# All 390 transposes on TensorE read and write through float32r views instead of float32

## The reference, cut to what matters

```python
def _conformer_layer(x, norm_g, w_in, dw_w, dw_b, ln_g, ln_b, w_out):
    h = _rms_norm(x, norm_g)
    a, b, z = jnp.split(h @ w_in, 3, axis=-1)
    y = _depthwise_causal_conv(a * jax.nn.sigmoid(b), dw_w, dw_b)
    y = jax.nn.silu(_layer_norm(y, ln_g, ln_b))
    return x + (y * jax.nn.silu(z)) @ w_out
...
def _diff_layer(x, k, v, ...):
    u = _rms_norm(x, norm_g) @ w_in
    q = _rms_norm(u[..., :DIFF_QK]...) ; z = u[..., DIFF_QK:]
    o = _rms_norm(_diff_attention(q, k, v, lam), subln_g) * (1.0 - lam_init)
    return x + (o * jax.nn.silu(z)) @ w_out
...
def hybrid_layer(x, cos, sin, ...):
    proj = rms_norm(x, pre_norm_w) @ w_in
    o_a = stick_breaking_attention(...) ; o_b = chunk_causal_softmax_attention(...)
    y = jnp.concatenate([o_a * silu(sb_gate), o_b * silu(mla_gate)], -1) @ w_out
    return x + rms_norm(y, post_norm_w)
```

## Time and profile before

| | |
|---|---|
| Time, median of 3 runs | 1269.71 us (1269.62 to 1270.36) |
| Span of the profiled execution | 1267.8 us |
| TensorE busy in it | 1259.6 us, 99% |
| Weight loads busy | 1052.1 us, 83% |
| VectorE, ScalarE, GpSimd busy | 791.8, 766.9, 204.6 us |
| Mean granted TensorE clock | 0.999 of full speed |

### The profile page before, as it was taken

The page is one execution under the profiler, slowest core; times in us unless marked ns, Lnnn a source line. Parts: engine busy times, 40 slices in busy tenths (PEclk is TensorE's granted clock), DMA queues, the critical chain, the costliest instruction groups (busy, mean ns, idle before and its releaser), DMA issues.

```text
span 1267.8 us, 16054 instructions
## 1 busy us (share of the span) xinstructions
PE 1259.6 (99%) x5936; PEld 1052.1 (83%) x5936; DVE 791.8 (62%) x1284; ACT 766.9 (60%) x1208; POOL 204.6 (16%) x148
## 2 busy tenths in 40 slices
PE   9999999999999999999999999999999999999998
PEld 8888888888888888888888888889988888888886
DVE  5498898476556665446677765555544445676545
ACT  5798798764557554445566674446644455666543
POOL 1499998900000000000000000000000000000000
PEclk9999999999999999999999999999999999999999
DMA  9898998944566666666555455567655556655563
GB/s 349 268 256 248 267 257 241 264 157 144 179 192 183 185 186 193 191 193 185 165 155 160 151 165 184 183 191 174 182 160 157 162 154 185 195 167 153 182 195 134
DMA packets 133564, 243.85 MB, mean 192 GB/s; under 512 B 12144, under 2 KB 22512, under 8 KB 133360
## 3 DMA queue, kind: packets, MB, share of 16 engines
q1 hardware_dynamic: 129600, 229.40, 58.2%
q0 software_dynamic: 3600, 13.11, 5.3%
q10 hardware_dynamic: 288, 0.32, 0.1%
HBM read 227.60 MB, written 2.10 MB: 181 GB/s over the span
## 4 chain that ended last, share of the span: by engine, by line
PE 97%; DVE 1%; ACT 1%; issue 0%; DVEq 0%; ACTq 0%
PE PS L1561 29%; PE PS L1563 29%; PE PS L1562 29%; PE PS L1494 3%; PE PS L1505 2%; PE PS L1690 1%; PE PS L1584 0%; PE PS L1586 0%; PE PS L1585 0%; PE PS L1623 0%; PE PS L1784 0%; PE PS L1754 0%; PE PS L1766 0%; PE PS L1643 0%; PE PS L1606 0%; PE PS L1612 0%
## 5 line engine op out<-in xcount | busy, mean ns | idle before, releaser
L1017 DVE TENSOR_TENSOR w_lo<-w_raw,w_hi 128x1024 fp32r<-128x1024 f32 (+1 forms) x339 | 411.1, 1214 | 354.0 <-ACT w_hi L549 353.1
L549 ACT ACTIVATE w_hi<-w_raw 128x1024 fp32r<-128x1024 f32 (+1 forms) x383 | 401.8, 1051 | 368.0 <-PE PS L1563 352.3
L1561 PE MATMUL PS<-w_hi,actB_hi 128*128 128x512 f32 (+1 forms) x752 | 298.8, 397 | 0.0
L1561 PE MATMUL PS<-w_hi,actA_hi 128*128 128x512 f32 x756 | 296.3, 392 | 0.0
L1563 PE MATMUL PS<-w_hi,actA_lo 128*128 128x512 f32 x756 | 294.6, 390 | 0.0
L1562 PE MATMUL PS<-w_lo,actA_hi 128*128 128x512 f32 x756 | 294.2, 389 | 0.0
L1563 PE MATMUL PS<-w_hi,actB_lo 128*128 128x512 f32 (+1 forms) x752 | 291.1, 387 | 0.0
L1562 PE MATMUL PS<-w_lo,actB_hi 128*128 128x512 f32 (+1 forms) x752 | 290.4, 386 | 0.0
L1563 PEld LDWEIGHTS PS<-w_hi,actA_lo 128*128 128x128 f32 x756 | 141.9, 188 | 30.1
L1561 PEld LDWEIGHTS PS<-w_hi,actA_hi 128*128 128x128 f32 x756 | 141.9, 188 | 29.3 <-DVE actA_lo L1032 0.3
L1562 PEld LDWEIGHTS PS<-w_lo,actA_hi 128*128 128x128 f32 x756 | 142.0, 188 | 29.1
(11 more groups left out here) (258 smaller groups left out, 1131.1 us busy)
## 6 DMA issues: line engine op xcount, KB each, us to landing
w_raw<-in_a_w_in SPq DMA_DIRECT2D x95, 512.0 KB, 5.7
w_raw<-in_w_in SPq DMA_DIRECT2D x88, 512.0 KB, 3.7
w_raw<-in_w_kv SPq DMA_DIRECT2D x64, 512.0 KB, 3.8
w_raw<-in_b_w_in SPq DMA_DIRECT2D x64, 512.0 KB, 3.7
w_raw<-in_a_w_out SPq DMA_DIRECT2D x32, 512.0 KB, 3.7
w_raw<-in_b_w_out SPq DMA_DIRECT2D x32, 512.0 KB, 3.7
w_raw<-in_w_out SPq DMA_DIRECT2D x32, 512.0 KB, 4.2
tap_products<-tap_products POOLq DMA_DIRECT2D x25, 512.0 KB, 8.3
```

The lines of the kernel that those rows point to most:

```text
L549: nc.scalar.activation(split_slot(u)[0], w_raw[:, RAW_SLOT[u], 0:2 * w], ACT.Copy)\
L1017: V.tensor_tensor(wl, w_raw[:, RAW_SLOT[u], 0:2 * w], wh.bitcast(F32), ALU.subtract)\
L1561: T.matmul(bank, ah, wh[:, kk, :], start=first and kk == 0, stop=False)
```

## The change

`ident_r`, a float32r copy of the identity, is made by GpSimd right behind the identity, and the wait ahead of unit 0 asks for it too. Each buffer that is turned gets a second name of type float32r at the same address (a tensor that is opened and closed right before the real one, or a slice of `aux_r`). All transposes go through `turn`, which reads the float32r names and writes PSUM through a float32r view. Number, shape, order and waits of TensorE's instructions are as before.

```diff
+        with nc.sbuf_tensor("x_res_r", [P, TT, D], F32R) as x_res_r:
+            pass
         x_res = sb("x_res", [P, TT, D])
...
         ident = sb("ident", [P, P])
+        ident_r = sb("ident_r", [P, P], F32R)
...
+            pool.wait_ge(S["ident_ready"], 1)
+            chain.tensor_copy(ident_r[:, :], ident[:, :]).then_inc(S["ident_ready"], 1)
             chain.memset(strict[:, :], 1.0)
...
+            def turn(out, src):
+
+                return T.transpose(out.bitcast(F32R), src, ident_r[:, :])
+
             def transpose_chunk(name, src, tiles=range(4)):
...
-                        ins = T.transpose(PS[:, 4 + i // 2, at:at + P], src(tok, i), ident[:, :])
+                        ins = turn(PS[:, 4 + i // 2, at:at + P], src(tok, i))
...
             def staged(buf):
-                return lambda tok, i: stage[:, buf, tok, i * P:(i + 1) * P]
+                return lambda tok, i: stage_r[:, buf, tok, i * P:(i + 1) * P]
...
-            pe.wait_ge(S["ident_ready"], 1)
+            pe.wait_ge(S["ident_ready"], 2)
...
-                            ins = T.transpose(PS[:, 6, i * P:(i + 1) * P], work[:, 0, i * P:(i + 1) * P],
-                                              ident[:, :])
+                            ins = turn(PS[:, 6, i * P:(i + 1) * P], work_r[:, 0, i * P:(i + 1) * P])
```

More of the change, by code:

```diff
@@ L263, in hybrid_program @@
         sb("w_raw_room", [P, RAW, 2 * NC])
+        with nc.sbuf_tensor("heads_out_r", [P, 4, TT, 2 * DH], F32R) as heads_out_r:
+            pass
         heads_out = sb("heads_out", [P, 4, TT, 2 * DH])
@@ L266, in hybrid_program @@
         w_lo = sb("w_lo", [P, PARTS, 2 * NC], F32R)
+        with nc.sbuf_tensor("stage_r", [P, 2, TT, NC], F32R) as stage_r:
+            pass
         stage = sb("stage", [P, 2, TT, NC])
+        with nc.sbuf_tensor("work_r", [P, 2, 384], F32R) as work_r:
+            pass
         work = sb("work", [P, 2, 384])
@@ L299, in hybrid_program @@
         conv = view(KT * (PAD + SEQ), KT, SEQ)
+        conv_r = aux_r[:, KT * (PAD + SEQ):KT * (PAD + 2 * SEQ)].rearrange("p (a b) -> p a b", a=KT)
         x_t = conv
         z_late = view(0, 2 * TT, NC)
+        z_late_r = aux_r[:, 0:2 * TT * NC].rearrange("p (a b) -> p a b", a=2 * TT)
         taps = view(KT * (PAD + 2 * SEQ), KT, TAPS)
@@ L317, in hybrid_program @@
         qu_stage = heads_out[:, 0:2, :, :].rearrange("p a b c -> p (a b c)").rearrange("p (t n) -> p t n", t=TT)
+        qu_stage_r = heads_out_r[:, 0:2, :, :].rearrange("p a b c -> p (a b c)").rearrange("p (t n) -> p t n", t=TT)
         qu_tmp = heads_out[:, 2:4, :, :].rearrange("p a b c -> p a (b c)")
@@ L1510, in staged @@
             def staged(buf):
-                return lambda tok, i: stage[:, buf, tok, i * P:(i + 1) * P]
+                return lambda tok, i: stage_r[:, buf, tok, i * P:(i + 1) * P]
             def rows(j):
-                return lambda tok, i: x_res[:, tok, j * NC + i * P:j * NC + (i + 1) * P]
+                return lambda tok, i: x_res_r[:, tok, j * NC + i * P:j * NC + (i + 1) * P]
             source = {}
@@ L1642, in _ @@
                             for i in range(4):
-                                ins = T.transpose(PS[:, 4 + tok, i * P:(i + 1) * P],
-                                                  conv[:, 4 * j + i, tok * P:(tok + 1) * P], ident[:, :])
+                                ins = turn(PS[:, 4 + tok, i * P:(i + 1) * P],
+                                           conv_r[:, 4 * j + i, tok * P:(tok + 1) * P])
                             ins.then_inc(S["stats_full"], 1)
@@ L1656, in _ @@
                     transpose_chunk(f"z{j}", staged(j) if j < 2 else
-                                    lambda tok, i: z_late[:, 2 * (j - 2) + tok, i * P:(i + 1) * P])
+                                    lambda tok, i: z_late_r[:, 2 * (j - 2) + tok, i * P:(i + 1) * P])
                 if C_OUT <= JUST_DONE.get(u - 2, 0) < C_K:
@@ L1694, in _ @@
                     pe.wait_ge(S["d_gated"], 2 * (j + 1))
-                    transpose_chunk(f"og{j}", lambda tok, i: heads_out[:, (2 * j + i // 2) % 4, tok,
-                                                                       (i % 2) * P:(i % 2 + 1) * P])
+                    transpose_chunk(f"og{j}", lambda tok, i: heads_out_r[:, (2 * j + i // 2) % 4, tok,
+                                                                         (i % 2) * P:(i % 2 + 1) * P])
                 if C_OUTB <= JUST_DONE.get(u - 2, 0) < C_CQ:
@@ L1708, in _ @@
                     for tok in range(TT):
-                        T.transpose(PS[0:ROT, 5, tok * P:(tok + 1) * P], stage[:, 1, tok, 256:320], ident[:, :])
+                        turn(PS[0:ROT, 5, tok * P:(tok + 1) * P], stage_r[:, 1, tok, 256:320])
                     for i in range(2):
@@ L1712, in _ @@
                             at = i * SEQ + tok * P
-                            ins = T.transpose(PS[:, 4, at:at + P], stage[:, 1, tok, i * P:(i + 1) * P],
-                                              ident[:, :])
+                            ins = turn(PS[:, 4, at:at + P], stage_r[:, 1, tok, i * P:(i + 1) * P])
                     ins.then_inc(S["t_full"], 1)
@@ L1722, in _ @@
                                 at, f = pair * SEQ + tok * P, (2 * j + pair) * P
-                                ins = T.transpose(PS[:, 4, at:at + P], qu_stage[:, tok, f:f + P], ident[:, :])
+                                ins = turn(PS[:, 4, at:at + P], qu_stage_r[:, tok, f:f + P])
                         ins.then_inc(S["t_full"], 1)
@@ L1748, in _ @@
                         for i in range(3):
-                            ins = T.transpose(PS[:, 7, i * P:(i + 1) * P], work[:, h % 2, i * P:(i + 1) * P],
-                                              ident[:, :])
+                            ins = turn(PS[:, 7, i * P:(i + 1) * P], work_r[:, h % 2, i * P:(i + 1) * P])
                         ins.then_inc(S["m_pt"], 1)
```

## The result

The changed kernel takes 1262.01 us (median, 1261.84 to 1262.53) beside 1269.95 us for the kernel before, timed again beside it (1269.71 us in the table above): a ratio of 0.9938, 95% interval 0.9925 to 0.9950. It is faster, by 7.9 us. The forecast was 16.1 us less, 1253.6 us; the gain is half of that, and the measured time lies just past the upper end of the range of 1251 to 1262. The number of the rival "a partly shortened load" was 1261.7 us.

What follows compares the result with a forecast made beforehand. TensorE was taken as the bound. 334 steps falling from 109 to 60 ns save 16.4 us, less 0.3 us lost on ScalarE: 16.1 us, from 1269.7 to 1253.6 us, range 1251 to 1262 us.

Steps and rivals of the forecast that it cites:

- a partly shortened load: Rival: float32r transposing load keeps part of the ordinary load's extra time; step 85 ns, 8.0 us less, 1261.7 us; chance 0.13.
- What bounds the kernel: Whole kernel: TensorE, busy 1259.6 of 1267.8 us and 97% of the chain, so time saved inside transpose runs is saved.
- The count: 390 transposes in 60 runs; 334 are followed by another transpose, each step saving 109 - 60 ns, 16.4 us in all.
- Matmul from two passes to one: Transposes' moving side: float32r drops one of two passes, step 109 to about 60 ns, record 273 to about 223 ns.
- The load: Weight load of a float32r transpose: taken at the low end, about 60 ns, with upper bound 108 to 120 ns.
- The last transpose of each run gives nothing: At the run's end: the ordinary load behind takes its 110 ns whatever the matmul does, so 56 transposes save nothing.
- Helpers and GpSimd: Outside TensorE: helper chains move along except 0.3 us lost; GpSimd's 4.4 us lead covers TensorE's 2.7 us gain until 255 us.
- The wait of the earlier trace: At 904.7 us on ScalarE, 0.24 us, behind two runs of 4 at line 1723: 0.3 us of gain lost.
- No change: Rival: load binds at its ordinary 108 ns, or the float32r view misses the instruction; 1269.7 us; chance 0.11.
- slower: Rival: load becomes the ordinary float32r one, pairs at 120 ns; 4.3 us more, 1274.0 us; chance 0.07.
- GpSimd would bind: Rival, from 50 to 255 us: GpSimd becomes the bound, 2.7 us of the gain go, 1256.3 us; inside the range.
- The load record stays at 140: Sign in the trace: transposes' load record stays 140 ns; 188 ns would mean the load rule held, time unchanged or worse.

Runs made afterwards that it cites:

- experiment 3: Changed kernel plus 296 float32r transposes with 64 load columns and 128 moving columns, overwritten by the real ones: 1280.63 us, ratio 1.0087 to before.
- Experiment 12: Changed kernel with the last transpose of each run in float32 again: 1261.16 us, ratio 0.9928 to before.
- experiment 8: Kernel before plus only GpSimd's float32r copy of the identity and TensorE's wait for it, transposes still float32: 1269.86 us, ratio 1.0002.
- experiment 7: Changed kernel plus 296 ordinary float32r products of 128 x 128 by 128 columns, not transposing: 1295.07 us, ratio 1.0201 to before.
- experiment 4: Changed kernel plus 296 float32r transposes of 64 rows, with 64 moving and 128 load columns: 1296.47 us, ratio 1.0211 to before.
- experiment 5: Changed kernel plus 296 float32r transposes of 64 x 64, load and moving columns both halved: 1288.30 us, ratio 1.0146 to before.
- experiment 6: Kernel before plus 296 float32 transposes of 64 rows, with 64 moving and 128 load columns: 1298.44 us, ratio 1.0228.
- experiment 9: Kernel before plus 296 float32 transposes of 32 rows, with 32 moving and 128 load columns: 1297.67 us, ratio 1.0216.

## Why the prediction was off by half

- **What bounds the kernel: right.** TensorE makes 96% of the chain, and the runs of transposes lost as much as the kernel did, 7.9 us.
- **The count: right.** 334 steps x (109 - 86) = 7.7 us (8.0 at 85 ns).
- **Matmul from two passes to one: right.** 225 ns for the record of one that doesn't wait, where 223 was forecast, and at most 60 ns of step once the load is halved (experiment 3).
- **The load: this is the term that failed.** It was taken at 60 ns and measured 84 to 86. The step of the argument was: plain float32 and float32r loads have the same record, 190 and 188 ns, so "it is the transpose that shortens it, not the type". Both halves were inferred from record lengths. For float32 the reading was right: 60 ns forecast, 62 or less measured, and about 50 less than the ordinary one's 112. For float32r it was not: transposing takes off 26 ns and not 50 (112 to 86), and the record of 140 ns doesn't show it. The range of bounds, 53 to 120, had held the value; the choice of the low end, and 0.69 for it, had no row behind it in which a float32r load of a transpose was seen. At 85 ns and not 60 a step saves 24 ns and not 49, and that alone is the missing half.
- **The last transpose of each run gives nothing: right in the count, not in the place.** Ordinary loads behind the run stay 0.11 us apart (110 and 108 ns), as forecast. But the step from the last transposing load to the ordinary one falls from 109 to 86 ns, and it is the first step of a run that gives nothing, 231 ns before and after. One step of each run is lost either way, so the count of 334 holds. Experiment 12 shows the same: what sets the time at the end is the last transposing load and then the ordinary one, so its *load* counts.
- **Helpers and GpSimd: right.** No wait of TensorE from GpSimd appeared between 50 and 255 us. The wait of the earlier trace rows grew by 0.07 us, not 0.3, and TensorE's wait for VectorE at 257 us went from 0.37 to 0.60. Together that is the 0.3 us of the forecast, mostly in another place. The copy of the identity cost nothing (experiment 8).
- **The rivals.** The partly shortened load was right with its mechanism and nearly to its number, 85 ns and 1261.7 us, though 85 was only a midpoint. It had 0.13. "No change" and "slower" both took the load of a float32r transpose to be an ordinary one. Ordinary ones take 112 ns (experiment 7) and it takes 84 to 86, so both are excluded; that the float32r view might not reach the instruction is excluded by the matmul's record, 225 ns and not 273. That GpSimd would bind didn't happen either.
- **The range.** Its upper end was a step of 86 ns with none of the 0.3 us for the helpers taken off, and 85 to 86 ns is what came: the edge stood on the value of the middle case, with no room behind it. Its lower end, 1251, is a step of 52 ns by the prediction's own sum and not 54.
- **The signs named in advance.** "The load record stays at 140" was to speak for the forecast. It came true and said nothing, because the record has that length at 62 and at 85 ns. "Matmul starts 60 ns apart" and "225 ns" hold for the first of a run alone. The chain's run of 8 (0.53 us expected, 0.64 measured) and TensorE's busy time (16 us less expected, 8.4 measured) did speak against it. A sign that decides would have been the distance of the loads in the middle of a run.

The Trainium skill had a number that fits better than the forecast: "TensorE: Matmul & The Clock Gate", section "Back-to-back issue gap", gives about 81 ns for sustained pairs of 128 columns, and the trace has 85 to 86 for float32r transposes. It isn't the pace of every such pair, however: with 128 moving columns, an ordinary float32r load makes it 112 ns (experiment 7) and half a transposing load 60 ns (experiment 3). The rule of "LDWEIGHTS (loading the stationary operand)" on the same page, columns divided by 1.2 per ns and so 107 ns for 128 columns, fits ordinary loads, measured at 108 to 112, and no transposing one. The section names no type; "in any type" was the prediction's reading of it.

## What to carry to other kernels

When a matmul gets cheaper, its weight load can be next, and what was hidden under the old matmul was never timed: find a place where it isn't hidden, or give both ends of its bounds real weight. A record's length compares columns within one type and mode; only the distance of the starts, in the middle of a run that doesn't wait, tells a pace. In this kernel float32r transposes of 128 x 128 go at 85 ns beside 109 in float32, bound by the load: a narrower load shortened the step (experiment 3) and a shorter matmul did not (experiment 4).

## What was not expected of the hardware

- A transposing load of 128 columns takes 84 to 86 ns in float32r and 62 or less in float32, with equal records (140 and 140 ns; 136 and 139 with 64 rows). Why the type matters is open. No run separates the type of the load from that of its matmul.
- Going from 128 rows to 64 or 32 and back cost 250 to 280 ns for each place (experiments 4, 5, 6, 9), and halving the columns alone cost nothing of the kind (experiment 3; 63 ns each by the time, 60 in the trace). Why is not shown: the first load of 64 rows comes 0.31 us later than a load of 128 rows does, with 0.35 us "issue" ahead of it, and the first load of 128 rows behind them is late again.
- A matmul's record contains its wait for weights: 225 ns for one that has them, 250 for one that is 25 ns early.
